# Two layers of a streaming encoder in float32 on one core: an eighteenth load slot, and another order of the first slots

## The reference

```python
for l in range(DEPTH):
    h = rms_norm(x, g_attn_norm[l])
    proj = h @ w_in[l]
    q_lat, kv_lat, k_rope, q_swa, k_swa, v_swa, gate_pre = jnp.split(proj, IN_OFFSETS, axis=-1)
    o_mla = mla_attention(q_lat, kv_lat, k_rope, g_q_norm[l], g_kv_norm[l], w_q_up[l], w_kv_up[l])
    o_swa = swa_attention(q_swa, k_swa, v_swa, sinks[l])
    gates = jax.nn.sigmoid(gate_pre + b_gate[l])
    merged = g_mla * (o_mla @ w_br_mla[l]) + g_swa * (o_swa @ w_br_swa[l])
    x = x + merged @ w_out[l]
    h = rms_norm(x, g_ffn_norm[l])
    x = x + (swiglu(h, ...) if l == 0 else moe_swiglu(h, ...))
return rms_norm(x, g_final)

def moe_swiglu(h, w_router, w_gate, w_up, w_down):
    top_vals, top_idx = lax.top_k(h @ w_router, 2)
    combine = one_hot(top_idx) weighted by softmax(top_vals)
    for e in range(8):
        y = y + combine[..., e:e + 1] * swiglu(h, w_gate[e], w_up[e], w_down[e])
```

## Time and profile before

| | |
|---|---|
| median of 3 runs | 1401.55 us |
| profiled execution, its own time | 1401.67 us |
| its span | 1399.8 us |
| busy PE / DVE / ACT / POOL | 1350.1 / 486.7 / 493.6 / 22.2 us |
| HBM read | 446.47 MB |
| granted TensorE clock | 0.998 of full speed |

### The profile page before, as it was taken

How to read it: one execution, slowest core, us unless ns; L and a number is a source line. 1 busy time by engine, 2 the same in 40 slices (tenths; PEclk the granted TensorE clock), 3 DMA queues, 4 the chain that set the end, 5 groups by cost and what they waited for, 6 DMA issues and landing times.

```text
span 1399.8 us, 21441 instructions
## 1 busy us (share of the span) xinstructions
PE 1350.1 (96%) x9122; PEld 699.4 (50%) x9122; DVE 486.7 (35%) x722; ACT 493.6 (35%) x842; POOL 22.2 (2%) x61
## 2 busy tenths in 40 slices
PE   9999999999999999999989999999889999999886
PEld 8887888888898785333322333333222233333221
DVE  5777855555666863111111111111111111111123
ACT  6566454344556644213222223113112113213112
POOL 1000000000000003000000000000000000000100
PEclk9999999999999999999999999999999999999999
DMA  9933655537554339999999999999999999999995
GB/s 350 347 113 121 204 179 189 180 120 242 169 199 136 143 122 421 410 421 420 409 420 408 420 420 421 409 421 421 409 421 421 406 421 421 409 420 420 419 422 216
DMA packets 95542, 456.33 MB, mean 326 GB/s; under 512 B 7656, under 2 KB 13304, under 8 KB 52432
## 3 DMA queue, kind: packets, MB, share of 16 engines
q1 hardware_dynamic: 91280, 443.13, 79.9%
q10 hardware_dynamic: 2704, 6.97, 1.5%
q0 software_dynamic: 1456, 4.79, 0.9%
HBM read 446.47 MB, written 8.39 MB: 325 GB/s over the span
## 4 chain that ended last, share of the span: by engine, by line
PE 73%; DMA 19%; DVE 3%; ACT 2%; issue 1%; SPq 1%; ACTq 0%; DVEq 0%
PE A L508 23%; PE DN L508 12%; PE A L497 7%; DMA raw_more<-in_moe_w_up 7%; PE A L499 7%; PE A L498 7%; DMA raw_more<-in_moe_w_gate 4%; DMA raw_more<-in_moe_w_down 4%; PE A L503 3%; DMA raw<-in_moe_w_down 2%; DMA raw<-in_moe_w_up 2%; PE DN L499 1%; PE DN L497 1%; PE DN L498 1%; PE DN L503 1%; PE T L2201 1%
## 5 line engine op out<-in xcount | busy, mean ns | idle before, releaser
L508 PE MATMUL A<-raw_more,heTf 128*32 128x512 f32 x2160 | 257.9, 594 | 4.2 <-DMA raw_more<-in_moe_w_up 1.9
L472 DVE TENSOR_TENSOR wlo<-raw,whi 128x2048 fp32r<-128x2048 f32 (+3 forms) x83 | 180.0, 2175 | 94.2 <-ACT whi L465 94.2
L465 ACT ACTIVATE whi<-raw 128x2048 fp32r<-128x2048 f32 (+3 forms) x83 | 150.8, 1821 | 99.3 <-PE A L499 56.5
L497 PE MATMUL A<-whi,hTh 128*128 128x512 f32 (+2 forms) x448 | 174.4, 389 | 1.5 <-DVE wlo L1137 0.9
L498 PE MATMUL A<-wlo,hTh 128*128 128x512 f32 (+2 forms) x448 | 170.0, 380 | 0.0
L499 PE MATMUL A<-whi,hTl 128*128 128x512 f32 (+2 forms) x448 | 170.0, 379 | 0.0
L1013 ACT ACTIVATE aTf<-T 128x384 f32<-128x384 f32 (+1 forms) x56 | 25.2, 450 | 381.1 <-PE T L2201 381.1
L508 PEld LDWEIGHTS A<-raw_more,heTf 128*32 128x32 f32 x2160 | 71.7, 110 | 160.7 <-issue 149.4
L508 PE MATMUL A<-raw,heTf 128*32 128x512 f32 x1200 | 150.3, 593 | 0.4 <-DMA raw_more<-in_moe_w_up 0.4
L1595 DVE TENSOR_TENSOR sg<-A,pT 96x512 f32<-96x512 f32 x35 | 24.0, 687 | 363.0 <-ACT pT L985 363.0
L508 PE MATMUL DN<-raw_more,aTf 128*32 128x512 f32 x1056 | 118.2, 593 | 0.4
(11 more groups left out here) (355 smaller groups left out, 1645.9 us busy)
## 6 DMA issues: line engine op xcount, KB each, us to landing
raw_more<-in_moe_w_gate SPq DMA_DIRECT2D x73, 1024.0 KB, 27.4
raw_more<-in_moe_w_up SPq DMA_DIRECT2D x72, 1024.0 KB, 27.3
raw_more<-in_moe_w_down SPq DMA_DIRECT2D x71, 1024.0 KB, 27.6
raw<-in_moe_w_down SPq DMA_DIRECT2D x41, 1024.0 KB, 27.4
raw<-in_moe_w_up SPq DMA_DIRECT2D x40, 1024.0 KB, 27.4
raw<-in_moe_w_gate SPq DMA_DIRECT2D x39, 1024.0 KB, 27.1
raw<-in_w_in SPq DMA_DIRECT2D x22, 1024.0 KB, 6.7
raw<-in_dense_w_down SPq DMA_DIRECT2D x11, 1024.0 KB, 5.0
```

The source lines that it names most:

```text
L465: nc.scalar.activation(split_slot(u)[0][:, :n], raw_of(u, e)[:, :n], ACT.Copy).then_inc(hi_done, 1)
L472: nc.vector.tensor_tensor(lo[:, :n], raw_of(u, e)[:, :n], hi[:, :n].bitcast(F32), ALU.subtract).then_inc(lo_done, 1)
L497: nc.tensor.matmul(o, hi, wh, start=start, stop=False)
L508: return nc.tensor.matmul(o[at * QUARTER:(at + 1) * QUARTER], tokens, w, start=start, stop=stop, tile_position=(0, at * QUARTER))
```

## The change

The change makes a slot 17 (`LOW`) of the second half of `o_o`, where `oTl` lay, and moves `aTf` to the free end of `pj` (behind `mg` and so behind slot 6). The semaphore `const_landed` is now that of the new slot, as other early loads already share those of other slots. The first 18 expert units are put into slots in another order: after slots 7 and 8 (unchanged) come 1, 2, 3, 4, then 17, 5, 6, 0, then 12, 15, 13, 16, 11, 14, then 9 and 10. The order before was 7, 8, 0, 1, 2, 3, 6, 4, 5, 11, 14, 12, 15, 13, 16, 9, 10.

```diff
-        aTf = place("aTf", [P, 2, 4, WIDE], F32, o_o + 8192)
         o_pj = used[0]
         pj = place("pj", [P, NB, C_GATE], F32)
         mg = place("mg", [P, NB, D], F32, o_pj)
+        aTf = place("aTf", [P, 2, 4, WIDE], F32, o_pj + 8192)
...
-            [o_pj, o_qT, o_kT, o_h, o_h + 4 * UNIT] + [o_w + 4 * UNIT * i for i in range(2 * S)])]
+            [o_pj, o_qT, o_kT, o_h, o_h + 4 * UNIT] + [o_w + 4 * UNIT * i for i in range(2 * S)] + [o_o + 8192])]
...
         W_SLOT = R + 5
+        LOW = W_SLOT + 2 * S
-        LANDED_EARLY = range(W_SLOT - 1, W_SLOT + 6)
+        LANDED_EARLY = range(W_SLOT - 1, LOW + 1)
-        const_landed = sem("const_landed")
+        const_landed = raw_landed[LOW]
...
-        FIRST_SLOTS = [R + 1, R + 2, 0, 1, 2, 3, R, 4, 5] + [W_SLOT + s + k for s in range(S) for k in (0, S)] + [R + 3, R + 4]
+        LAST_SPLIT = [u % R for u in range(UM - R, UM)]
+        FREED_W = [W_SLOT + u % S + k for u in range(UM - S, UM) for k in (0, S)]
+        FIRST_SLOTS = [R + 1, R + 2] + LAST_SPLIT[:4] + [LOW] + LAST_SPLIT[4:5] + [R] + LAST_SPLIT[5:] + FREED_W + [R + 3, R + 4]
...
                     if held is None and slot == R:
                         sp.wait_ge(mg_T[1], 4)
+                    elif held is None and slot == LOW:
+                        sp.wait_ge(unit_used, at[1, "out"])
```

## The result

The changed kernel took 1391.38 us, the median of 4 runs (1390.66 to 1392.47), against 1401.55 us before (4 runs, 1401.47 to 1401.76). The ratio is 0.9928 with a 95% interval of 0.9913 to 0.9944: faster by 10.2 us, or 0.7%. The forecast was 1389.3 us in a range of 1386.0 to 1394.5. A later set of runs on another occasion gave 1391.73 us against 1401.64, 9.9 us.

What follows compares the result with a forecast made beforehand. DMA was taken as the bound over the eight experts. A 13.8 us lead, cut to 12.3 by expert 0's slots, gave 1401.67 - 12.3 = 1389.4 us, 1389.3 for the median; range 1386.0 to 1394.5 us.

Steps and rivals of the forecast that it cites:

- What bounds the kernel: Over the eight experts: DMA engines full at 417 GB/s, 2.5 us a load; PE alone would end 54 us earlier.
- The gap, and what holds it: From 491 to 514 us: DMA moves 1 GB/s, as the third load waits for slot 0 until 513.80 us.
- The lead at 541 us: At PE's first use in expert 0: 17.8 loads moved instead of 12.3, a lead of 5.5 loads or 13.8 us.
- What expert 0 gives back: Inside expert 0: slots cap the stream at 59 loads, cutting the lead from 13.8 us to 12.3 us, 4.9 loads.
- A second count: End of expert 0: the load issued at 648.96 lands at 653.8 instead of 668.0 us, 14.2 us as upper end.
- The slot's own worth: End of expert 0: the eighteenth slot raises the cap from 58 to 59 loads, worth 2.5 us; the order 9.8.
- What is late next: Expert 1 becomes limited by PE, which gains some 10 us; slots don't bind again at the end of expert 3.
- The signs: Expected in the profile after: issue times from 485 us, landings of 5 to 8 us in expert 0, last landing near 1373.5.
- That the slots don't bind: Expert 0: the stream stays under the cap of 59, so all 13.8 us stay: 1387.8 us; chance 10%.
- PE as the bound: Experts: PE sets the time and an earlier stream only fills slots, so the kernel stays at 1401.6 us; chance 4%.
- The slower case: From 491 to 537 us: loads beside projection, norm and routing delay PE's start; 16 us of delay gives 1405 us; chance 4%.
- The lag in a thin queue: Expert 0: a nearly empty queue lags by two loads, 5 us, leaving 7.3 us gained: 1394.4 us; chance 14%.

Runs made afterwards that it cites:

- nineteenth slot: Changed kernel with one more slot, over `xn`, joining the rotation at g = 26: 1390.25 us, ratio 0.992; the changed kernel beside it took 1391.73 us.
- half loads in expert 0: Changed kernel with eight loads of expert 0 bringing only half their bytes: 1391.54 us; the kernel before with the same edit: 1393.9 us.
- those in expert 5: Changed kernel with eight loads of expert 5 bringing only half their bytes: 1381.39 us.

## Why the prediction was right, point by point

**What bounds the kernel: right.** DMA's place in the stream was named as the bound against a busy PE and a chain that is 73% PE. Half the bytes of eight loads in a wide expert took off the full 10 us.

**The gap, and what holds it: right.** The load of slot 0 held back those behind it. With it third, as before, the rest of the new order is worth nothing; with it tenth the loads went out at the predicted times to within 0.2 us: 485.0, 494.9, 500.8, 507.4, 509.6, 513.7 and 519.7.

**The lead at 541 us: right**, 5.6 loads against the predicted 5.5.

**What expert 0 gives back: right in kind, too small in size.** This is the term of the sum that was off. I had put it at 13.8 - 12.3 = 1.5 us, and it measured 2.5 + 1.4 = 3.9; less the 0.3 us by which the lead at 541 us was larger, that is the difference between 12.3 us and 10.2. I put the lead after expert 0 at 4.9 loads, from a capacity of 59.5 against a limit of 59, and counted 0.1 load for what is still under way. Taken from the windows, some 4.6 loads were left at 550 us and 4.05 at 660. Three things were missed.

First, that the loads asked for 98% of the stage's DMA time said nothing of when. The last of the 18 first loads landed at 527.87 + 15.3 = 543.2 us, while PE's uses let the next ones out only at 540.94, 542.66 and 546.09 us, so the queue was all but empty from 541 us on. Second, I let the lead be final at 651 us, when the queue was not yet full again; from 651 to 660 us the rate is 375 GB/s against 421 before. Third, I had taken the slot limit as if the stream could press right against it, while some loads come in pairs whose second waits for PE (the two issues that begin at 648.92 us take 2.91 us). The nineteenth slot shows that the loss near 650 us goes away with one slot more, and that it is 1.5 us. What happens in the engines meanwhile it doesn't show.

A second count, by the landing of one load, had given 14.2 us as the upper end. The load issued at 648.92 us landed 5.6 us later, at 654.5, against 668.0 before: 13.5 us, 3.2 more than was left at the end.

**The slot's own worth: nearly right.** Of the sum I had given 2.5 us to the slot and 9.8 to the order. Measured were 1.9 and 8.3: each term is somewhat less, the order's too, since its part of the lead goes through the same stage.

**What is late next: right, but for PE's gain.** Expert 1 after the change has no wait of PE for a load in it, where before the waits of PE from 651 to 728 us came to 3.0 us, all for loads. I had said that PE would gain some 10 us in expert 1; it gained about 6 (its first matmul of expert 2 starts at 728.74 us instead of 734.72), which doesn't bear on the sum. The queue then filled up again, with 26.0 us to landing for a load issued at 697 us, and it didn't run dry at the end of expert 3 (418 to 424 GB/s from 945 to 970 us, and about 30 us to landing at 950 to 962 us).

**The signs: one failed.** I had named landing times of 5 to 8 us in expert 0. They were 5.6 to 6.3 at its ends, but 13.3 us at 569 us and still 8.6 at 633 us. The last landing moved by 10.3 us, close to the 10 under which I would have called myself wrong.

**The rivals.** That the slots don't bind is refuted by the half loads in expert 0. PE as the bound is refuted by those in expert 5. The slower case is refuted by PE's start, which did not come later, with DMA at 221 GB/s in the stretch where it had been idle. The lag in a thin queue comes nearest to what happened (1391.4 us lies between the forecast, 1389.3, and its 1394.4), and it is not refuted. The range held both, so the time alone can't tell them apart, and the windows show a part of each. From 541 to 550 us the share is 0.87 where it was 1.02 before, 1.35 us of idle engines; the other 1.15 of the 2.5 us are a lower rate while they count as busy. From 640 to 660 us nearly all of the 1.4 us is of that second kind (share 1.00 against 1.01). These are the 5 us with the lowest rate, after and before:

```profile
655.00:660.00 5.00, 5.00 (x26) 1.72 (x24) 1.66 (x3) 1.75 (x3) 0.00 (x0) 1.00 0.99 351
655.00:660.00 5.00, 5.00 (x26) 1.62 (x24) 1.48 (x3) 1.82 (x3) 0.00 (x0) 1.00 1.02 423
```

Here the queue isn't empty: by their issues and landings three or four loads are always under way (the one issued at 651.6 lands at 657.2 us, those of 653.21 and 654.92 at 662.5 and 665.2). The share can't decide between waiting and a slower rate, as the half loads show. The nineteenth slot can't either, since it takes away both. So that expert 0 gives back 3.9 us is shown, and that it is a matter of slots; how much of it is waiting and how much a slower thin queue stays open.

The rule of the Trainium skill that I set against the forecast (page "DMA: Bandwidth & Descriptors", section "Bandwidth": 1 MB at 341 GB/s, for a DMA issued from GpSimd, while these loads are issued from SP) is thus not decided by this: from 640 to 660 us the thin queue moved 391 GB/s, above the rule and below the 420 of a full one.

## What to carry to other kernels

When loads go out in program order on one queue, the slot that comes free last should stand last. The first load that waits holds back all behind it, and as long as it stood third here, neither a slot more nor another order behind it was worth anything. A buffer more pays only in a stage in which the stream has caught up with its consumer; here it was worth 1.5 to 2.5 us, at most one transfer. The time from issue to landing helps to tell which case it is: 5 to 6 us at the ends of expert 0, near the 4.8 of a lone load, where slots limit, and 16 to 28 us where bandwidth does. In between (8.6 to 13.3 us inside expert 0, with other traffic beside) it doesn't decide, and there the rate against the consumer's pace says more. And a lead won ahead of a slower consumer has to be followed to the end of that stage, with the windows cut where the slots are full, since a mean load of 98% can hide a thin start.

## What was not expected

- DMA traffic at 221 GB/s beside the output projection, the norm and the routing cost these stages nothing that can be seen (PE's first expert matmul at 537.24 us, before 537.42).
- Half an order change was worth 6.7 us, the other half 0, and both 10.2 (with the slot in all three).
- From 655 to 660 us, with three or four loads under way, the DMA engines show a share of 0.99 at 351 GB/s. A high share at a low rate isn't special to a thin queue. Both kernels have it from 670 to 680 us with a long queue too (loads land after 19 to 21 us and 26 to 28 us), after and before:

```profile
670.00:680.00 10.00, 10.00 (x52) 3.38 (x48) 2.05 (x3) 2.20 (x4) 0.00 (x0) 1.00 1.02 375
670.00:680.00 10.00, 10.00 (x50) 3.39 (x48) 2.04 (x3) 2.20 (x4) 0.00 (x0) 1.00 1.02 378
```

Why the engines count as busy without moving more stays open in both places.
